# Opening of a two-layer block on one core: twelve constant products in place of eight, three small transfers issued later

## What is computed

```python
h = rms_norm(x, pre_mix_norm[l])
proj = jnp.einsum('bsd,dc->bsc', h, w_in[l])
att_q, att_k, att_v, gdn_qkv, gdn_z, gdn_a, gdn_b = jnp.split(proj, split_points, axis=-1)
...
beta = jax.nn.sigmoid(b.astype(jnp.float32))
g = -jnp.exp(A_log.astype(jnp.float32)) * jax.nn.softplus(
    a.astype(jnp.float32) + dt_bias.astype(jnp.float32))
...
l_own = l_own + rel_bias[:, rel_bucket(d_own)]
l_own = jnp.where(d_own >= 0, l_own, -jnp.inf)
```

## Time and profile before

| | before |
|---|---|
| median of 3 runs | 906.03 us (905.59 to 906.92) |
| span of the profiled execution | 905.7 us |
| PE busy | 894.0 us, 99% |
| DVE busy | 604.6 us, 67% |
| ACT busy | 456.3 us, 50% |
| POOL busy | 95.4 us, 11% |

### The profile page before, as it was taken

The page is one execution under the profiler, slowest core; times in us unless marked ns, Lnnn a source line. Parts: engine busy times, 40 slices in busy tenths (PEclk is TensorE's granted clock), DMA queues, the critical chain, the costliest instruction groups (busy, mean ns, idle before and its releaser), DMA issues.

```text
span 905.7 us, 12742 instructions
## 1 busy us (share of the span) xinstructions
PE 894.0 (99%) x5426; PEld 761.5 (84%) x5426; DVE 604.6 (67%) x723; ACT 456.3 (50%) x554; POOL 95.4 (11%) x94
## 2 busy tenths in 40 slices
PE   8999999999999999999999999999999999999997
PEld 8989888788888887888888878778788888888885
DVE  5899896676566557778857564655556566664665
ACT  6675564564444447555443355443355555444443
POOL 2041231100000000000126310110100000000000
PEclk9999999999999999999999999999999999999999
DMA  9654324246555543654564544344454356445531
GB/s 331 248 205 147 126 63 170 88 163 230 198 194 198 197 190 140 221 186 149 208 221 167 185 159 167 140 186 184 171 200 142 141 194 234 171 183 216 186 140 46
DMA packets 26088, 160.45 MB, mean 177 GB/s; under 512 B 3576, under 2 KB 4232, under 8 KB 8240
## 3 DMA queue, kind: packets, MB, share of 16 engines
q1 hardware_dynamic: 23616, 153.40, 46.3%
q0 software_dynamic: 2272, 6.24, 2.1%
q10 hardware_dynamic: 144, 0.00, 0.0%
HBM read 158.57 MB, written 2.63 MB: 178 GB/s over the span
## 4 chain that ended last, share of the span: by engine, by line
PE 81%; DVE 13%; ACT 3%; issue 2%; DMA 1%; POOL 0%; POOLq 0%; SPq 0%; DVEq 0%; ACTq 0%
PE banks L501 33%; PE banks L469 21%; PE banks L472 10%; DVE t_wl L1620 5%; PE banks L573 3%; PE banks L529 2%; PE banks L424 2%; PE banks L443 2%; PE banks L1019 2%; DVE t_cout L1649 2%; PE banks L412 1%; PE banks L765 1%; ACT t_wh L1139 1%; PE banks L969 1%; PE banks L1101 1%
## 5 line engine op out<-in xcount | busy, mean ns | idle before, releaser
L1620 DVE TENSOR_TENSOR t_wl<-t_raw,t_wh 128x2048 fp32r<-128x2048 f32 x136 | 312.4, 2318 | 117.0 <-ACT t_wh L1139 115.8
L469 PE MATMUL banks<-t_hx,t_wh 128*128 128x512 f32 x992 | 312.0, 396 | 0.0
L1139 ACT CAST t_wh<-t_raw 128x2048 fp32r<-128x2048 f32 x136 | 255.6, 1907 | 12.3 <-DMA t_raw<-in_W 7.6
L472 PEld LDWEIGHTS banks<-t_hx,t_wl 128*128 128x128 f32 x992 | 186.3, 188 | 43.7
L472 PE MATMUL banks<-t_hx,t_wl 128*128 128x256 f32 x992 | 194.9, 278 | 0.0
L469 PEld LDWEIGHTS banks<-t_hx,t_wh 128*128 128x128 f32 x992 | 153.3, 189 | 2.4
L501 PE MATMUL banks<-t_wh,t_hx 128*128 128x512 f32 x320 | 102.0, 395 | 0.0
L501 PEld LDWEIGHTS banks<-t_wh,t_hx 128*128 128x128 f32 x320 | 59.5, 188 | 12.7 <-issue 0.6
L501 PE MATMUL banks<-t_wl,t_hx 128*128 128x512 f32 x160 | 61.1, 390 | 0.0
L2251 POOL TENSOR_TENSOR t_st<-t_st,t_half 128x1 f32<-128x1 f32 (+1 forms) x18 | 10.6, 591 | 435.5 <-DVE t_st L1649 425.8
L1471 ACT COPY t_hold<-banks 128x512 f32<-128x512 f32 x28 | 16.4, 585 | 67.4 <-PE banks L472 56.2
(11 more groups left out here) (322 smaller groups left out, 1340.4 us busy)
## 6 DMA issues: line engine op xcount, KB each, us to landing
t_raw<-in_W SPq DMA_DIRECT2D x139, 1024.0 KB, 4.8
t_raw<-in_W SPq DMA_DIRECT2D x8, 256.0 KB, 6.5
t_raw<-in_W SPq DMA_DIRECT2D x4, 512.0 KB, 8.8
skew<-scr POOLq DMA_DIRECT2D x1, 1536.0 KB, 13.0
t_cout<-in_xT SPq DMA_DIRECT2D x4, 256.0 KB, 5.6
t_x<-in_x SPq DMA_DIRECT2D x2, 512.0 KB, 9.7
t_tab<-in_tab POOLq DMA_DIRECT2D x1, 640.0 KB, 7.4
out<-t_xt SPq DMA_DIRECT2D x2, 320.0 KB, 2.3
```

The costliest lines, as they stand in the source:

```text
L469: e.matmul(bank[b + c], M.wh[:, h, wk], M.hx[:, k, :, :].rearrange("p a s -> p (a s)"), start=k == 0, stop=False)
L472: m = e.matmul(bank[b + c][:, 0:S], M.wl[:, h, wk], M.hh[:, k, :], start=False, stop=k == 7)
L1139: e.copy(M.wh[:, h, :], M.raw[:, r, :]).then_inc(q.sem, q.tick(("hi", i)))
L1620: e.tensor_tensor(M.wl[:, h, :], M.raw[:, r, :], M.wh[:, h, :].bitcast(F32), ALU.subtract).then_inc(q.sem, q.tick(("lo", i)))
```

## The change

PE makes twelve constant products where it made eight. On POOL, the issues of `onehot` and `rbT` move behind the product for the gates, and the issue of `neg` moves behind the two powers of the norm and behind the issue of `tab`. Nothing else differs; DVE, ACT and SP have the same instructions in the same order.

```diff
@@ -647,7 +647,7 @@
-            constants(8)
+            constants(12)
@@ -2272,16 +2272,16 @@
             e.memset(M.half[:], -0.5).then_inc(q.sem, q.tick("half"))
             e.memset(M.cin[:, :, 0:3], 0.0).then_inc(q.sem, q.tick("pad"))
-            e.dma_start(M.oh, A["onehot"]).then_inc(LD["onehot"], 16)
-            e.dma_start(M.ng, A["neg"]).then_inc(LD["neg"], 16)
-            e.dma_start(M.rb, A["rbT"]).then_inc(LD["rbT"], 16)
             q.wait_dma(LD["wab"])
             q.wait_dma(LD["pre"])
             o = M.wab.rearrange("p (k j) -> p k j", k=8)
             tt(o, o, bc(par("pre_mix"), 32), ALU.mult, "wab")
+            e.dma_start(M.oh, A["onehot"]).then_inc(LD["onehot"], 16)
+            e.dma_start(M.rb, A["rbT"]).then_inc(LD["rbT"], 16)
             rstd("in", 0)
             rstd("in", 1)
             e.dma_start(tab[:], A["tab"].rearrange("p (a n) -> p a n", n=128)).then_inc(LD["tab"], 16)
+            e.dma_start(M.ng, A["neg"]).then_inc(LD["neg"], 16)
             q.wait_ge(DV, "row")
```

## The result

| | runs | median us | lowest to highest |
|---|---|---|---|
| before | 6 | 906.23 | 905.59 to 906.92 |
| changed | 6 | 909.77 | 909.11 to 910.52 |

The ratio is 1.0037 (95% interval 1.0027 to 1.0046): the change makes the kernel slower by 3.5 us. The forecast was 906.6 us and no measurable difference.

The account below looks back on a forecast made before the run. PE was taken to bound the kernel until 24.4 us, then DVE until beyond 49.89; -2.3 (clock) + 3.0 (wait for `neg`) = +0.7 us gave 906.4 us for the profiled execution, 906.6 as median, range 904.3 to 908.1.

Parts of the forecast that it names:

- Twelve products cost nothing in the wait before unit 0: PE's opening: the four added products lie in its 1.79 us wait for ACT's first rounding, ending about 6.5 us.
- PE is 2.3 us early: Gates' products on PE: with the clock higher from 7 us, they end at 13.95 us instead of 16.23.
- -2.3 (clock): Term of the sum: 2.3 us gained at the opening by PE's clock rising at 7 us instead of 12.6.
- The tokens land at 19.1 us, whatever PE does: Tokens' second half: lands at 19.1 us, so the norm's second power is ready at 21.1 us.
- `roots` "just fits": `roots` wants the norm's second power at 21.15 us, 2.3 us ahead of its old time; ready at 21.1.
- `neg` keeps its place behind `tab` and lands 0.2 us after it: POOL's queue: `neg` lands at 28.7 us, so DVE stands still from 25.7 and `row` starts 0.7 us later.
- The bound on the other side: `neg` as quick as later 128 KB transfers (2.4 us): there at 24.1, `row` at 25.7, a gain of 2.3 us.
- It goes through to PE: DVE's 0.7 us delay reaches PE, which waits 1.7 us at unit 4 and 1.7 us for `t_dU` in unit 5.
- -2.3 + 3.0: The sum: 2.3 us gained by the clock, 3.0 us lost in DVE's new wait for `neg`, net +0.7 us.
- Rival (b): PE's opening: extra products don't raise the clock sooner, `neg` lands at 29.2; +1.2 us, 907.1 us; chance 0.11.
- (a): `neg` on POOL's queue is quick: landing at 27.2 gives 905.1 us, before 25.7 gives 903.6; chance 0.20.
- (c): PE's clock falls in its new waits at 37 and 49 us, costing 3 us: 909.6 us; chance 0.07.

Follow-up runs that it names:

- the second profile of before: The kernel before, profiled once more with no edit: 905.86 us with a span of 904.1 us.

## Why the prediction was wrong, step by step

- **Twelve products cost nothing in the wait before unit 0:** right. They end at 6.48 (said: 6.5), and alone they make no difference (0.9998).
- **PE is 2.3 us early, and the sum's "-2.3 (clock)":** this is the step that failed. Against the profile it was nearly right (2.0 us: 15.16 in the earlier trace rows, 13.14 after), but that execution had the late clock, and its time stands at the upper end of its kernel's runs. The second one has the higher clock with eight products already and starts the gates' products at 13.24. The gain over the runs of the kernel before is 0.0, and at most 1.0 by the interval (ratio 0.9998, 0.9989 to 1.0007), not 2.3. The prediction noted that no row showed the moment of the rise to differ between runs; now two profiles of one kernel do. The sign was there: the prediction took the 0.3 us between the profile's span, 905.7, and the median of three runs, 906.03, for the time around the span. That time is 1.8 us, so the profiled execution had taken 907.5, above the highest of the three runs (906.92).
- **The tokens land at 19.1 us, whatever PE does, and `roots` "just fits":** 0.8 to 0.9 us off. The second half landed at 9.6 + 10.4 = 20.0 us in the changed kernel and at 8.8 + 11.1 = 19.9 in the second profile of before. So `tab` was issued at 21.94 and not at 21.1, and `neg` at 22.54. That is 0.8 of the 1.0 us by which `neg`, landing at 29.7, missed its forecast of 28.7.
- **`neg` keeps its place behind `tab` and lands 0.2 us after it:** right, and it is the mechanism of the loss. DVE's wait was 3.35 us (said: 3.0). The bound on the other side, a small transfer as quick as the 2.4 us of later ones, was not reached even with nothing ahead of it (5.1 us).
- **It goes through to PE:** right. PE waited 1.6 us at unit 4 (said: 1.7), and for `t_dU` 1.1 us in three waits (said: 1.7 in one).
- **The sum:** -2.3 + 3.0 should have been 0.0 + 3.35, and on the measured 906.23 that gives 909.6. The range ended at 908.1, because it was drawn about the landing of `neg` and left the other term, the gain, without a case in which usual runs had it already. Rival (b), by which the extra products bring no earlier clock, was near, but had the clock late in both kernels where it is early in both, and so put the loss at 1.2 us, from the same late execution. Rivals (a) and (c) did not happen: right behind both of PE's waits, at 40 and at 52 us, the matmuls of 256 columns are 0.12 us apart.

## What to carry to other kernels

One profiled execution can be an unusual one: lay its time, not its span, beside the runs, and ask whether a gain repairs the kernel or only that execution. A small transfer landed the later the more stood ahead of it on its queue; and what it costs is not its delay but the list behind the instruction that waits for it, so look whether that instruction can stand where the wait is over.

## What had not been expected

- In the two profiles whose clock rose late, the second half of the tokens landed at 19.0 to 19.1 us; in the second profile of before and in the changed kernel, both with an early rise, at 19.9 to 20.0, and in the other nine, all with an early rise, at 19.5 to 20.7. Between the two profiles of before SP's issues differ by at most 0.5 us (15.36 against 15.83), and nothing in them explains it. Why a faster start goes with later tokens stays open; it takes back part of what the early clock gives.
- `neg` took 5.1 us for 12 KB at 22 us with nothing of its queue ahead of it, about the 5.5 us of the first microseconds and twice the 2.4 of the bias tables (`t_T<-skew`) later.
- All nine profiles with twelve or sixteen products have the higher clock by the end of unit 0's first piece. None of the 44 runs of the four kernels with twelve products and no wait for `neg` has a span above 905.0 us, while 6 of the 73 runs of the kernel before beside them reach 905.5 or more. Twelve products may take away these longest executions; no profile of one of those 6 is there to show it.
